# One decoder pair in a single launch: who empties the query blocks, where the decay sums stand, and how wide ff1's moving operand is

## The chip, the cores and the metric

The kernel runs on one core of a Trainium2 chip. The metric is the device time of one execution in microseconds. Three runs of the kernel before took 1574.8, 1575.58 and 1578.62 us; the median is 1575.58 us.

## The reference

The input x is 256 tokens of width 1024 (`SEQ, D = 256, 1024`). It passes a first block of two layers and then a second block of one layer.

A layer of the first block is an RMS norm, a projection, three kinds of mixing (latent attention, selected-key attention, retention), an output projection, and a feed-forward part with `D_FF = 4096`:

```python
hid = square(relu(rms_norm(x) @ w_ff1))     # 256 x 4096
x   = x + hid @ w_ff2
```

The second block projects the normed rows to q, k, v (3 x 768 columns), to the RWKV columns (1824) and to gates (2048). It then computes:

```python
# attention: 3 patterns x 4 heads, scores + bias, softmax, values, w_att_out
w_log = -softplus(-(w0 + tanh(xw) @ w_up)) - 0.5
decay = exp(-exp(w_log)); a = sigmoid(a0 + xa @ a_up); g = sigmoid(xg) @ g_up
# a recurrence over tokens (wkv7_scan): state = state * decay + ... ; out = state @ r
mixed = gates[:D] * y_att + gates[D:] * y_rwkv
x = x + mixed @ w_out
x = x + hierarchical_moe(rms_norm(x))       # 32 experts, top 2 of one group
```

The recurrence is not run token by token. The kernel forms running sums of the log decay within tiles of 128 tokens (the decay sums), takes their exponentials, scales r, k, a, b by them, and turns the recurrence into matmuls and a triangular inverse (the core).

## The kernel before, in words

All five engines run one written-out program each, tied by semaphores. TensorE's results go to eight PSUM banks of 512 words. Every use of a bank is a unit with a name, a bank (or a run of banks) and the engine that empties it, "A" for ScalarE or "V" for VectorE. `layer_plan()` (first block) and `second_plan()` (second block) list the units in TensorE's order. `begin` waits until the bank's previous unit is emptied, `finish` reports it full. So the order is written by hand, and a bank that is emptied late stops TensorE.

Weights come in pieces. SyncE's queue loads a raw piece, ScalarE rounds it to a high part (L1753), GpSimd or VectorE subtracts to get the low part (L878), and TensorE multiplies high x high, high x low and low x high (`product`, L1032 to L1034). A high part may be written only when TensorE has finished the piece 3 places before (first block) or 4 places before (second block).

ff1 works in 8 blocks b of 512 hidden columns for each layer, each block in two units j of 256, each unit in two halves f of 128 columns: for each of 8 k, three matmuls with 128 x 128 weights as the stationary operand and 256 tokens as the moving one. Its units rotate over banks 0 to 3. VectorE empties a unit of 128 x 512 with a maximum against zero (L2365) and squares it (L2367); ScalarE rounds it (L1910), VectorE subtracts (L2373), and ff2 of that block comes one block later. The order on TensorE is ff1(b), ff2(b-1).

The second block starts with `project("rw")`, then the query, key and value columns in five blocks (`QKV_BLOCKS`, four of 512 columns and one of 256, four weight pieces each, two units each: one for each tile of 128 tokens). Units of tile 0 are emptied by VectorE (L2440), units of tile 1 by ScalarE. VectorE first works through the token shift (L2433, L2435, L2437: three operations of 3648 words a partition, which signal `pm_ready`) and only then comes to the first of the query units. The banks are (1, 2, 3, 0), so the fifth unit (block 2) needs the first one emptied.

After the projection the LoRA rows are passed through sigmoid and tanh by ScalarE (L1950, L1951), transposed by TensorE (L1359 to L1361), emptied by ScalarE (L1954, L1955) and multiplied (L1368, L1370, L1371). Then come the gate columns, the transposes of q and k (L1381), and the attention.

The attention has 8 units (two tiles by four heads of three patterns). In round i TensorE makes the scores of i (L1392, L1396), transposes the probabilities of i-1 (L1404), and multiplies the values of i-2 (L1414). VectorE takes the maximum (L2513), ScalarE the exponential (L1976), and it empties the transposed probabilities into one buffer, `att_p`, for which it waits until the values of i-2 are finished.

Behind the attention stand the decay sums: four sums (L1422), eight one-column products in one unit (`sdec`, L1425 and L1426), exponentials on ScalarE (L1992, L1993, L1996), scaling on VectorE (L2529 to L2534, signal `scaled`), 8 units of 4 transposes (L1433), emptied by ScalarE (L2004), the transposed attention (L1440), and its output product `yatt` (L1021). Then the core starts (L1457). GpSimd waits for `scaled`, issues three DMAs of router weights (L2138 to L2140), and forms a product and fills.

The experts (MoE) end the program.

## Time and profile before

| what | value |
|---|---|
| median of three runs | 1575.58 us |
| the profiled execution's own time | 1577.1 us |
| its span | 1575.3 us |
| PE busy | 1489.3 us (95%) |
| DVE busy | 692.7 us (44%) |
| ACT busy | 543.9 us (35%) |
| POOL busy | 443.7 us (28%) |
| mean granted TensorE clock | 0.97 of full speed |

The profile is one execution of the program. PE is TensorE's matmuls, PEld its weight loads, DVE is VectorE, ACT is ScalarE, POOL is GpSimd, SP is SyncE. L12 is line 12 of the kernel. The row of a matmul tells its start and its length, and matmuls overlap: what one costs in a stream is the distance from its start to the next one's. PEclk 1.00 is 2.4 GHz and 0.50 is 1.2 GHz. A bracket at the end of a row is idle time of that engine before it, and who ended it.

### The profile page before, as it was taken

Reading aid. Unit: us, or ns where it says so; the run is one execution under the profiler, and the core shown is the slowest. Engines: PE = TensorE matmul, PEld = TensorE weight load, DVE = VectorE, ACT = ScalarE, POOL = GpSimd, SP = SyncE. Lnnn points to the kernel's source line nnn. Section 1 sums busy time; section 2 is a strip of 40 time slices with the busy share of each in tenths; the row PEclk is TensorE's granted clock in tenths of the full one; section 3 lists DMA queues with packets and bytes.
Section 4 is the critical chain, followed back from the end, with each engine's and each line's share of the span. In section 5 each row is a group of like instructions: output and inputs, shape, how many; then the busy total and the mean of one; then the engine's idle time right before and its main releaser. Section 6 shows DMA issues by size and latency. Waiting matters only on the chain.

```text
span 1575.3 us, 21537 instructions
## 1 busy us (share of the span) xinstructions
PE 1489.3 (95%) x8270; PEld 1087.3 (69%) x8270; DVE 692.7 (44%) x1070; ACT 543.9 (35%) x816; POOL 443.7 (28%) x160
## 2 busy tenths in 40 slices
PE   7989999998989999999979989999899999999997
PEld 6778899987778899987766768974445435444442
DVE  3785465564775475554316625553221111212111
ACT  5546543344646533335434431112111111111111
POOL 3372343434362444437886311100000000000000
PEclk9999999999989999999998979999999999999999
DMA  6442355554332355556763601026599999999995
GB/s 235 141 133 76 108 188 194 180 197 146 121 133 76 134 174 201 180 195 195 235 203 111 227 5 55 1 107 290 215 419 427 429 428 428 425 422 422 428 427 226
DMA packets 44426, 351.91 MB, mean 223 GB/s; under 512 B 5187, under 2 KB 7151, under 8 KB 19759
## 3 DMA queue, kind: packets, MB, share of 16 engines
q1 hardware_dynamic: 43646, 349.37, 58.0%
q8 instruction: 61, 1.00, 0.3%
q10 hardware_dynamic: 576, 1.13, 0.2%
q0 software_dynamic: 112, 0.17, 0.1%
q14 instruction: 31, 0.25, 0.0%
HBM read 347.71 MB, written 1.07 MB: 221 GB/s over the span
## 4 chain that ended last, share of the span: by engine, by line
PE 71%; DVE 8%; DMA 8%; issue 6%; DVEq 2%; ACT 2%; POOL 1%; POOLq 0%; SPq 0%; ACTq 0%
PE psum L1032 13%; PE psum L1033 12%; PE psum L1034 12%; PE psum L1652 12%; DMA ring<-in_w_expert_up 7%; PE psum L1679 5%; PE psum L1021 3%; PE psum L1611 3%; PE psum L1620 1%; PE psum L1100 1%; PE psum L1484 1%; DVE arena L2163 1%; DVE arena L2206 1%; DVE stat L2216 1%; PE psum L1119 1%
## 5 line engine op out<-in xcount | busy, mean ns | idle before, releaser
L878 POOL TENSOR_TENSOR weights_split<-weights_raw,weights_split 128x2048 fp32r<-128x2048 f32 (+4 forms) x108 | 389.6, 3620 | 428.8 <-ACT weights_split L1753 428.7
L1753 ACT ACTIVATE weights_split<-weights_raw 128x2048 fp32r<-128x2048 f32 (+4 forms) x154 | 243.3, 1584 | 283.3 <-PE psum L1034 283.0
L1652 PE MATMUL psum<-ring,arena 128*64 128x512 f32 x976 | 229.2, 604 | 11.2 <-DMA ring<-in_w_expert_up 10.1
L1652 PEld LDWEIGHTS psum<-ring,arena 128*64 128x64 f32 x976 | 74.4, 139 | 148.7 <-issue 148.7
L1032 PE MATMUL psum<-weights_split,h_split 128*128 128x512 f32 (+3 forms) x400 | 154.9, 387 | 15.8 <-DVE arena L2440 6.4
L1033 PE MATMUL psum<-weights_split,h_split 128*128 128x512 f32 (+3 forms) x400 | 153.0, 382 | 0.0
L1034 PE MATMUL psum<-weights_split,h_split 128*128 128x512 f32 (+3 forms) x400 | 152.7, 382 | 0.0
L1032 PE MATMUL psum<-weights_split,hidden_split 128*128 128x512 f32 (+1 forms) x384 | 151.6, 395 | 0.0
L1033 PE MATMUL psum<-weights_split,hidden_split 128*128 128x512 f32 (+1 forms) x384 | 150.1, 391 | 0.0
L1034 PE MATMUL psum<-weights_split,hidden_split 128*128 128x512 f32 (+1 forms) x384 | 149.7, 390 | 0.0
L1032 PE MATMUL psum<-h_split,weights_split 128*128 128x256 f32 x512 | 145.2, 284 | 1.4 <-DVE weights_split L878 1.4
L1034 PE MATMUL psum<-h_split,weights_split 128*128 128x256 f32 x512 | 144.9, 283 | 0.0
L1033 PE MATMUL psum<-h_split,weights_split 128*128 128x256 f32 x512 | 144.9, 283 | 0.0
L878 DVE TENSOR_TENSOR weights_split<-weights_raw,weights_split 128x2048 fp32r<-128x2048 f32 (+2 forms) x46 | 107.1, 2332 | 28.5 <-ACT weights_split L1753 27.8
L1679 PE MATMUL psum<-arena 128*64 128x512 f32 x512 | 113.4, 595 | 0.0
L1032 PEld LDWEIGHTS psum<-weights_split,h_split 128*128 128x128 f32 x400 | 77.4, 194 | 34.2 <-issue 13.2
L1032 PEld LDWEIGHTS psum<-h_split,weights_split 128*128 128x128 f32 x512 | 98.2, 192 | 2.5 <-DVE weights_split L878 1.8
L1033 PEld LDWEIGHTS psum<-h_split,weights_split 128*128 128x128 f32 x512 | 98.2, 192 | 0.5
L1034 PEld LDWEIGHTS psum<-h_split,weights_split 128*128 128x128 f32 x512 | 98.2, 192 | 0.0
L2373 DVE TENSOR_TENSOR hidden_split<-arena,hidden_split 128x512 fp32r<-128x512 f32 x32 | 85.8, 2681 | 15.2 <-ACT hidden_split L1910 15.2
L2794 DVE TENSOR_TENSOR arena<-psum,arena 128x512 f32<-128x512 f32 x16 | 11.1, 692 | 184.0 <-PE psum L1652 184.0
L2804 DVE SCALAR_TENSOR_TENSOR y_parts<-psum,stat,y_parts 128x512 fp32r<-128x512 f32 x32 | 24.0, 751 | 145.8 <-ACT y_parts L2057 145.8
(371 smaller groups left out, 2185.7 us busy)
## 6 DMA issues: line engine op xcount, KB each, us to landing
weights_raw<-in_layer_w SPq DMA_DIRECT2D x94, 1024.0 KB, 4.8
arena<-in_w_expert_down SPq DMA_DIRECT2D x32, 2048.0 KB, 13.3
ring<-in_w_expert_up SPq DMA_DIRECT2D x32, 2048.0 KB, 16.8
ring<-in_w_expert_gate SPq DMA_DIRECT2D x29, 2048.0 KB, 16.1
weights_raw<-in_second_w SPq DMA_DIRECT2D x44, 512.0 KB, 4.2
arena<-in_w_expert_gate SPq DMA_DIRECT2D x3, 2048.0 KB, 9.1
weights_raw<-in_layer_w SPq DMA_DIRECT2D x6, 768.0 KB, 4.1
ring<-in_w_out SPq DMA_DIRECT2D x2, 2048.0 KB, 17.1
```

The source lines that it names most:

```text
L878: eng.tensor_tensor(W.part(j, 1, n), W.raw(j, n), W.part(j, 0, n).bitcast(F32), ALU.subtract).then_inc(W.lo[W.pieces[j][1]], 1)
L1021: ins = pe.matmul(bank[:, 0:n], lhs(i), w[:, i, :], start=(i == 0), stop=(i == k - 1))
L1032: pe.matmul(out, a[0], b[0], start=first, stop=False)
L1033: pe.matmul(out, a[0], b[1], start=False, stop=False)
L1034: return pe.matmul(out, a[1], b[0], start=False, stop=last)
L1100: pe.matmul(bank[:, j * nk:(j + 1) * nk], qT_, kT_, start=True, stop=False)
L1611: ins = pe.matmul(psum[:, 6 + i, kk * P:(kk + 1) * P], xn2[:, t, k * P:(k + 1) * P], take[par][:, t, :, :].rearrange("p j n -> p (j n)"), ...
L1652: ins = pe.matmul(bank[half(j), :], xe[h][:, k, half(j)], w[j][:, k, :], start=(k == 0), stop=(k == KD - 1))
L1679: ins = pe.matmul(bank[half(j), :], hidT[:, f, half(j)], w[j][:, f, c * 512:(c + 1) * 512], start=(f == 0), stop=(f == D_EXP // P - 1))
L1753: act.activation(W.part(j, 0, w), W.raw(j, w), ACT.Copy).then_inc(W.hi, 1)
L2373: dve.tensor_tensor(part[1], hid_sq[i % 4], part[0].bitcast(F32), ALU.subtract).then_inc(hid_ready.sem, 1)
L2804: units.emptied_by(("y", h, c), dve.scalar_tensor_tensor(part[:, 1, :], bank, gate_slot, part[:, 0, :].bitcast(F32), mul, sub))
```

## The change

1. ff1: the three matmuls of one k become two. The high part of the weights multiplies both parts of the tokens in one matmul of 512 columns, into a bank of its own for each f; the low part multiplies the high tokens into the first 256 columns. A unit now has two banks, (0, 1) or (2, 3). VectorE empties it with a sum of two (1024 words in, 512 out), and one operation takes the maximum and squares.
2. Query blocks 0 and 1: both units are emptied by ScalarE.
3. The LoRA rows' sigmoid and tanh stand behind query block 2 on ScalarE, their transposes ahead of the last query block on TensorE.
4. The decay sums and `sdec` stand inside the attention's rounds; `sdec` (the one-column sums) in two halves. The exponential of a sum is written in place in PSUM, and VectorE scales from there. Values of the attention take bank 6 (before 6 and 7). The last attention unit has its own `att_p` and its own banks.
5. The 8 units of transposes are emptied by ScalarE and VectorE in turn; the transposed attention stands behind the sixth; `yatt` takes banks 4, 5, 7, 0 (before 2, 3, 4, 1).
6. The three router DMAs on GpSimd are issued after the second of the core's four starts.

```diff
-        plan += [("ff1", 2 * b + j, (2 * b + j) % 4, "V") for j in range(2)]
+        plan += [("ff1", 2 * b + j, ((0, 1), (2, 3))[j], "V") for j in range(2)]
...
+CUMS = ("cum_excl", "cum_incl") * T
+CUM_AT = {2 * j + 1: j for j in range(len(CUMS))}
...
-    plan += interleave("qkv", PROJ_QKV, (1, 2, 3, 0), "VA")
-    plan += interleave("loraT", T, (4, 5), "A")
+    qkv = [(*unit[:3], "A" if unit[1] < 2 * T else unit[3]) for unit in interleave("qkv", PROJ_QKV, (1, 2, 3, 0), "VA")]
+    plan += qkv[:-T] + interleave("loraT", T, (4, 5), "A") + qkv[-T:]
...
-            plan.append(("PT", i - 1, (4, 5), "A"))
+            plan.append(("PT", i - 1, (4, 5) if i < NA else (0, 1), "A"))
+        if i == 1:
+            plan.append(("sdec", 0, 6, "A"))
         if i >= 2:
-            plan.append(("O", i - 2, (6, 7)[i % 2], "V"))
-    plan += interleave("cum", 2 * T, (0, 1, 2, 3), "AV")
-    plan += interleave("sdec", 1, (4,), "A")
-    plan += interleave("rwT", 8, (5, 6, 7, 0), "A")
-    plan += interleave("attT", 1, (1,), "A")
-    plan += interleave("yatt", 2 * T, (2, 3, 4, 1), "V")
+            plan.append(("O", i - 2, 6 if i <= NA else 4, "V"))
+        if i in CUM_AT:
+            plan.append(("cum", CUM_AT[i], 7, "V"))
+    rwT = interleave("rwT", 8, (2, 3, 5, 7, 0, 1, 6, 2), "AV")
+    plan += rwT[:6] + interleave("attT", 1, (3,), "A") + rwT[6:]
+    plan += interleave("yatt", 2 * T, (4, 5, 7, 0), "V")
...
+        att_p = [area(28736, 768), att_s[0]]
...
-                        ins = product(bank[:, f * SEQ:(f + 1) * SEQ], [part_[:, k, f * P:(f + 1) * P] for part_ in w],
-                                      [hTp[:, which, k, :] for which in range(2)], k == 0, k == KD - 1)
+                        pe.matmul(both.rearrange("p (w s) -> p w s", w=2), w[0][:, k, f * P:(f + 1) * P], hTp[:, :, k, :],
+                                  start=(k == 0), stop=False)
+                        ins = pe.matmul(both[:, 0:SEQ], w[1][:, k, f * P:(f + 1) * P], hTp[:, 0, k, :], start=False, stop=(k == KD - 1))
...
+                if i < 2:
+                    bank = units.begin(("sdec", 0)) if i == 0 else units.bank(("sdec", 0))
+                    for c in range(i * PAIRS // 2, (i + 1) * PAIRS // 2):
+                        pe.matmul(bank[:, c:c + 1], bufR[:, 0, c * P:(c + 1) * P], second("halves")[:, 1:2], start=True, stop=False)
+                        ins = pe.matmul(bank[:, c:c + 1], bufR[:, 1, c * P:(c + 1) * P], second("halves")[:, 0:1], start=False, stop=True)
...
+                if i in CUM_AT:
+                    j = CUM_AT[i]
+                    bank = units.begin(("cum", j))
+                    units.finish(("cum", j), pe.matmul(bank, second(CUMS[j]), bufR[:, j // 2, :], start=True, stop=True))
...
+            act.wait_ge(preproc_done, 1)
             for i in range(NA + 1):
+                if i == 2:
+                    empty(("sdec", 0), sdec, PAIRS, ACT.Exp)
+                if i - 1 in CUM_AT:
+                    j = CUM_AT[i - 1]
+                    bank = units.wait_full(("cum", j))
+                    if CUMS[j] == "cum_incl":
+                        act.activation(bufK[:, j // 2, :], bank, ACT.Exp, scale=-1.0)
+                        act.drain()
+                    act.activation(bank, bank, ACT.Exp).then_inc(cum_exp, 1)
...
-                    if i >= 2:
+                    if 2 <= i < NA:
                         units.wait_full(("O", i - 2))
-                    empty(("PT", i - 1), att_p[:, 0:n], n)
+                    empty(("PT", i - 1), att_p[(i - 1) // (NA - 1)][:, 0:n], n)
...
-                        units.emptied_by(("ff1", i), dve.tensor_scalar(hid_sq[i % 4], bank, 0.0, None, ALU.max), "V")
+                        units.emptied_by(("ff1", i), dve.tensor_reduce(sq.rearrange("p (f s) -> p f s", f=2),
+                                                                       bank.rearrange("p f w s -> p f s w"), AX.X, ALU.add), "V")
                         dve.drain()
-                        dve.tensor_tensor(hid_sq[i % 4], hid_sq[i % 4], hid_sq[i % 4], ALU.mult)
+                        dve.scalar_tensor_tensor(sq, sq, 0.0, sq, ALU.max, ALU.mult)
...
-            for b, (c, w) in enumerate(QKV_BLOCKS):
+            for b, (c, w) in list(enumerate(QKV_BLOCKS))[2:]:
...
+            def scale_rw(j):
+                t = j // 2
+                dve.wait_ge(cum_exp, j + 1)
+                bank = units.bank(("cum", j))
+                if CUMS[j] == "cum_excl":
+                    units.emptied_by(("cum", j), dve.tensor_tensor(bufA[:, t, :], bank, bufA[:, t, :], mul), "V")
+                else:
+                    units.emptied_by(("cum", j), dve.tensor_tensor(bufR[:, t, :], bank, r_[:, t, :], mul), "V")
+                    dve.tensor_tensor(bufB[:, t, :], bufB[:, t, :], bufK[:, t, :], mul)
+                    dve.drain()
+                    dve.tensor_tensor(bufK[:, t, :], bufK[:, t, :], k_[:, t, :], mul)
+                    dve.drain()
+                    dve.sem_inc(scaled, 1)
...
+                if i - 1 in CUM_AT:
+                    scale_rw(CUM_AT[i - 1])
...
+            for j in (1, 3, 5, 7):
+                bank = units.wait_full(("rwT", j)).rearrange("p (c s) -> p c s", c=PAIRS)
+                units.emptied_by(("rwT", j), dve.tensor_copy(rwT[j % 4][:, :, j // 4 * P:(j // 4 + 1) * P], bank), "V")
```

## Rows read from the trace of the kernel before

**Rows 1.** The page's first part: busy time of each engine.

```profile
PE 1489.3 (95%) x8270; PEld 1087.3 (69%) x8270; DVE 692.7 (44%) x1070; ACT 543.9 (35%) x816; POOL 443.7 (28%) x160
```

**Rows 2.** The page's costliest groups: ff1's matmuls (count, busy, mean, idle before).

```profile
L1032 PE MATMUL psum<-h_split,weights_split 128*128 128x256 f32 x512 | 145.2, 284 | 1.4 <-DVE weights_split L878 1.4
```

**Rows 3.** Timeline of TensorE, end of an ff1 block to the next: start, length, operation.

```profile
639.81 0.28 PE L1034 MATMUL psum<-h_split,weights_split 128*128 128x256 f32 x1
...
648.21 0.40 PE L1032 MATMUL psum<-weights_split,hidden_split 128*128 128x512 f32 x1
...
659.12 0.28 PE L1032 MATMUL psum<-h_split,weights_split 128*128 128x256 f32 x1
```

**Rows 4.** Busy time by engine in a stretch of the feed-forward part.

```profile
560.00:640.00 80.00, 80.00 (x503) 72.69 (x502) 45.21 (x27) 31.11 (x22) 33.43 (x8) 1.00 0.57 196
```

**Rows 5.** Timeline of all engines in the feed-forward part.

```profile
603.58 0.69 DVE L2365 TENSOR_SCALAR arena<-psum 128x512 f32<-128x512 f32 x1 [0.92 <-PE psum L1034]
...
605.57 4.62 POOL L878 TENSOR_TENSOR weights_split<-weights_raw,weights_split 128x2048 fp32r<-128x2048 f32 x1 [6.90 <-ACT weights_split L1753]
```

**Rows 6.** Timeline of VectorE: a reduction of 768 words from PSUM.

```profile
900.63 0.96 DVE L2513 TENSOR_REDUCE stat<-psum 128x1 f32<-128x768 f32 x1 [2.94 <-PE psum L1396]
```

**Rows 7.** Timeline of TensorE: it resumes with query block 2.

```profile
792.68 0.77 PE L1032 MATMUL psum<-weights_split,h_split 128*128 128x512 f32 x1 [6.39 <-DVE arena L2440]
```

**Rows 8.** Timeline of GpSimd, the weight pieces of that time.

```profile
781.98 12.10 POOL L878 TENSOR_TENSOR weights_split<-weights_raw,weights_split 128x1024 fp32r<-128x1024 f32 x2
...
794.05 7.09 POOL L878 TENSOR_TENSOR weights_split<-weights_raw,weights_split 128x1024 fp32r<-128x1024 f32 x3
```

**Rows 9.** Timeline of VectorE, the last operation of the token shift.

```profile
785.91 5.96 DVE L2437 TENSOR_TENSOR arena<-arena 128x3648 f32<-128x3648 f32 x1
```

**Rows 10.** Three stretches by engine; the third number from the end is the granted clock.

```profile
794.00:796.00 2.00, 2.00 (x6) 1.52 (x6) 0.00 (x0) 0.00 (x0) 2.00 (x2) 0.50 0.48 172
...
830.00:832.00 2.00, 2.00 (x3) 0.49 (x3) 1.29 (x2) 0.00 (x0) 0.00 (x0) 0.50 0.81 225
...
926.00:928.00 2.00, 2.00 (x3) 0.67 (x2) 0.00 (x0) 0.00 (x0) 0.00 (x0) 0.50 0.00 0
```

**Rows 11.** Timeline of TensorE, the LoRA transposes and products.

```profile
826.19 0.33 PE L1359 MATMUL psum<-shared_c,arena 128*128 128x128 f32 x1 [3.49 <-ACT arena L1951]
...
827.87 2.08 PE L1368 MATMUL psum<-arena 64*128 64x512 f32 x4 [0.81 <-ACT arena L1955]
...
837.76 1.12 PE L1371 MATMUL psum<-arena 32*128 32x512 f32 x2
```

**Rows 12.** Timeline of TensorE from the transposes of q and k to the core.

```profile
883.72 2.78 PE L1381 MATMUL psum<-shared_c,arena 128*128 128x128 f32 x24
...
897.21 1.08 PE L1392 MATMUL psum<-arena,phase_c 128*128 128x512 f32 x2
898.21 1.13 PE L1396 MATMUL psum<-arena 64*128 64x256 f32 x4
...
918.26 0.84 PE L1404 MATMUL psum<-shared_c,arena 128*128 128x128 f32 x6 [1.28 <-ACT arena L1921]
...
922.00 2.82 PE L1414 MATMUL psum<-arena 128*128 128x64 f32 x12 [0.90 <-ACT arena L1921]
924.61 6.20 PE L1422 MATMUL psum<-arena,phase_c 128*128 128x512 f32 x8
930.64 0.28 PE L1425 MATMUL psum<-phase_c,arena 128*128 128x1 f32 x2
...
935.40 5.92 PE L1433 MATMUL psum<-shared_c,arena 128*128 128x128 f32 x32 [2.91 <-DVEq L2535]
...
942.69 7.10 PE L1021 MATMUL psum<-ring,hTs 128*128 128x512 f32 x16 [0.94 <-ACT hTs L1921]
949.73 8.86 PE L1457 MATMUL psum<-arena 64*128 64x128 f32 x80
```

**Rows 13.** Timeline of ScalarE: an exponential of 512 words.

```profile
928.42 0.60 ACT L1992 ACTIVATE arena<-psum 128x512 f32<-128x512 f32 x1 [6.48 <-PE psum L1422]
```

More of the change, by code:

```diff
@@ L1335, in _, with project @@
             _, _, _, part2 = split_products(PW, units, hTp2, second_piece, 0)
-            def project(stage, blocks):
-                for b, (_, w) in enumerate(blocks):
+            def project(stage, blocks, which=slice(None)):
+                for b, (_, w) in list(enumerate(blocks))[which]:
                     for i in range(4):
@@ L1405, in _ @@
                     units.finish(("PT", i - 1), ins)
+                if i < 2:
[3 more added lines that the diff above has]
+                        ins = pe.matmul(bank[:, c:c + 1], bufR[:, 1, c * P:(c + 1) * P], second("halves")[:, 0:1], start=False, stop=True)
+                    if i:
+                        units.finish(("sdec", 0), ins)
                 if i >= 2:
@@ L1441, in _ @@
             units.finish(("attT", 0), ins)
+            turn_rw(range(6, 8))
             w = weights(("att_out", 0))
```

105 lines of the change are left out of this document (41 added, 64 removed).

## The prediction

> **What bounds the kernel now.** I read the page's busy times first: TensorE is busy for 1489.3 us of 1575.3 [rows 1], so a change pays only where it takes work off TensorE or closes one of its gaps. Next came the stretches by engine: in the feed-forward part TensorE is busy for 80.00 of 80 us at clock 1.00, VectorE for 45.21, GpSimd for 33.43 [rows 4]; only TensorE's own work counts there. Then the timeline of TensorE through the second block, where the reader is to look for the brackets: a wait of 6.39 us on VectorE among the query blocks [rows 7], 3.49 and 0.81 us around the LoRA transposes [rows 11], and 1.28, 0.90, 2.91 and 0.94 us between the attention and the core [rows 12]. Last the granted clock: behind each of these gaps it is 0.50, the level of 1.2 GHz [rows 10]. The experts behind this shift as a whole: their loads are released by TensorE's last units of the second block.
>
> **Part 1, ff1.** In a stream a matmul of 256 columns costs (648.21 - 639.81) / 70 = 120.0 ns, one of 512 columns (659.12 - 648.21) / 48 = 227.3 ns [rows 3]. There are 512 groups of three [rows 2]. A group costs 3 x 120.0 = 360 ns before; after, 227.3 + 120.0 = 347.3 ns if the new matmul runs as ff2's do. The saving is 12.7 x 512 = 6.5 us. Bounds: columns alone, at half of 227.3 for the 256 too, give 341 ns, a gain of 9.7 us. The other end: the new moving operand is two runs of 256 words far apart, and so is that of the bias product, which takes 898.21 - 897.21 = 1.00 us for 512 columns where contiguous operands take (949.73 - 942.69) / 8 = 0.88 [rows 12]. At that ratio 227.3 becomes 258, the group 378 ns, and ff1 loses 9.4 us. I take 6.5: ff2 is the neighbour in the same stretch, and the bias product also follows a change from 64 to 128 rows, which can explain its 0.12 us.
>
> The Trainium skill, "TensorE: Matmul & The Clock Gate", section "Back-to-back issue gap", speaks for less: it puts N / 2.4 + 2.5 ns between full-clock matmuls, so that one matmul fewer saves about 2.5 ns; that estimate is 1.3 us for 512 groups. The rows show about 13 ns beyond the columns on each, and the sum goes by them.
>
> VectorE gets more work for each unit: a sum over 1024 words in place of 0.69 us [rows 5]. At the rate of the 768-word reduction (0.96 us [rows 6]) it is about 1.25 us, so +0.6 a unit, +1.1 a block. A block lasts 22.4 us (32 x 0.360 + 48 x 0.2273) and VectorE is busy for 45.21 / 80 = 57% of it, 12.7 us: it becomes 13.8. Even twice the price of the sum is covered. Two pairs of banks in place of four banks: a unit's pair is asked for again two units later, at the earliest 5.5 us after it was full (ff1(0) to ff1(1)), against 1.25 us for the emptying. The weights' chain runs 2% faster: GpSimd's piece starts at 605.57 and takes 4.62 us [rows 5], done at 610.2, and is needed when the two pieces now being multiplied (about 11 us from 603.3) are through, at 614. Cost nothing.
>
> **Part 2, query blocks 0 and 1.** The wait of 6.39 us goes, but another stands behind it. While VectorE does its token shift, GpSimd's low parts take 6.05 us each (two in 12.10) where the next three take 7.09 / 3 = 2.4 [rows 8]. By the count of pieces these two are the first and second of query block 2. So TensorE, which is through with block 1 at 792.68 - 6.39 = 786.3, waits for the first until 788.05, multiplies it (12 matmuls, 2.8 us) until 790.9, and waits for the second until 794.1. From there three pieces at 2.8 us end at 802.5. Before, the block started at 792.68, with ten matmuls at half speed [rows 10], and ended at 805.9: 3.4 us saved if the clock holds. Idle for 5 of 8 us, it hardly will; half speed for one to three pieces' worth costs 1.2 to 3 us. I take 2.0, ends 0.4 and 3.4. The end of the token shift (785.91 + 5.96 = 791.87 [rows 9]) does not move. ScalarE's two more units of 0.7 us fall where it waits for TensorE.
>
> **Part 3, LoRA.** Before, the last query block ends at 822.7 and the gates start at 837.76 + 1.12 = 838.9 [rows 11]: 16.2 us, in which the products run from 827.87 at half speed (11.0 us [rows 10, 11]). After, sigmoid and tanh are done under query block 3, the six transposes cost 6 x 0.116 = 0.7 us at full clock (24 in 2.78 [rows 12]), and their emptying lies under the last query block (5.6 us of matmuls). The products follow without a gap at full clock: six slots of 0.88 us, 5.2 us. Saved 16.2 - 5.2 - 0.7 = 10.3; ends 5 (the clock falls all the same) and 10.8. What moves on ScalarE (2 us with its table load, 1.1 us of copies) stands ahead of weight pieces that TensorE wants 5 us later or more. VectorE's long chain up to the attention, which is done only 1.3 us before the first maximum, hangs on a square root behind gate block 0, so it keeps its place relative to TensorE.
>
> **Parts 4 to 6, attention to core.** In the rounds of the second tile TensorE has no gap, so what moves in costs its own time: four sums at 0.88 and eight one-column products at about 0.2. The first three sums and `sdec` delay the last scores by 2.6 + 1.8 - 0.5 = 3.9 us (0.5 falls into a gap of the first rounds). The fourth sum fills 0.9 of the 1.28 us before the last transposes. Its two exponentials (0.60 each [rows 13]) delay the last probabilities on ScalarE by 1.4 us, but these no longer wait for the values before, so that the 0.90 goes and about 0.1 is left. Then, from the last scores' end at 914.8 + 3.9 = 918.7: values, fourth sum and last transposes by 922.9, values at full clock by 925.5. The first tile's transposes are ready; the second tile's scaling ends at 923.3 + 3 x 0.69 (as [rows 5]) = 925.6. Nine units of transposes at 0.44 take until 929.4, with the attention's emptying under the last two; `yatt` takes 7.0 us [rows 12] to 936.4. The core's first unit now wants the bank of the last `yatt` unit, emptied 0.9 us later: 937.3. Before it started at 949.73 [rows 12]: 12.4 us saved. Of that the sums at half speed [rows 10] and the waits of 2.91 and 0.94 are most. Ends: 8 (low clock through transposes and half of `yatt`) and 13.5.
>
> VectorE's scaling inside a round (0.7 to 2.1 us) stands ahead of emptying the values and of the next maximum. Queued behind it are those two, and TensorE asks for the value bank a round (5.3 us) later; VectorE has 1.8 us of other work a round. The wait for `preproc_done` on ScalarE costs nothing, the first maximum is behind it on VectorE anyway. The router DMAs go into a time when GpSimd waits 39 us for the core's second tile; they are read over 80 us later. In the old place they delayed nothing that TensorE waited for: 0.
>
> **Sum.** 6.5 + 2.0 + 10.3 + 12.4 = 31.2 us. The profiled execution took 1577.1 us, so the same execution becomes 1545.9; it is 1.5 above the median of the runs, which gives 1544.4.
>
> **Rivals.**
> A. The clock stays low from the attention to the core. Here gaps shrink, but the run of transposes grows. Price from rows: 36 transposes at twice 0.11 cost 4 us, and two or three units of `yatt` at half speed 3 to 4: 1551. Against it: of the 32 transposes from 935.40 the last run fast again, the following matmuls at full speed [rows 12], so a stretch of transposes did bring the clock up. The Trainium skill, "TensorE: Matmul & The Clock Gate", section "Part 4: PE-mode transpose", says that transposes don't count as busy for the clock. By that rule this rival would hold; the trace disagrees.
> B. The split operand is no faster than two matmuls of 256 (240 ns) or up to 258: ff1 gains 0 or loses up to 9.4 us: 1551 to 1560. For it only the bias product.
> C. Slower than before: the two-run operand streams at half rate, 455 ns for 512 columns. 512 x (455 + 120 - 360) = 110 us more, less 24.7 from the second block: 1661. It decides from 240 + 24.7 / 0.512 = 288 ns on. Against it: the bias product's operand is of that shape and costs 1.00 us, not 1.76 [rows 12].
> D. The LoRA part does not close (ScalarE comes late with the weights of the gates): 5 us less, 1550. Against it the 5 us of lead above.
>
> **Chances.** Forecast 0.64 (its own range 1540 to 1549), A 0.12, B 0.13, D 0.06, C 0.03, and 0.02 that the second block's gains are eaten by a stall I do not see. About 0.3% (4.7 us) is what a measurement can tell. Faster 0.95, same 0.02, slower 0.03. The range takes A, D and half of B, and downwards 9.7 and 3.4 in place of 6.5 and 2.0: 1538 to 1555.
>
> **What would show it.** ff1: starts of a pair 347 ns apart in sum, TensorE still at 80 of 80 us. Query block 2: two waits on GpSimd (1.8 and 3.1 us) in place of one on VectorE. LoRA: no gap, products in 5.2 us, clock 1.00. From the end of q and k's transposes to the core about 51 us in place of 63.2. The prediction is wrong if the 512-column matmuls stand over 240 ns apart, or if VectorE's row L2373 grows into ff2's start.

## The result, and the profile after

The kernel after the change takes 1560.87 us (median of 4 runs, 1554.68 to 1562.0), the kernel before 1575.86 on the same chip. The ratio is 0.9903, 95% interval 0.988 to 0.9925: faster by 15 us, or 1%. I had forecast 1544.4 with a range of 1538 to 1555. The direction is right, but only half of the 31.2 us came, and the time lies outside the range.

The page's busy times of the kernel after stand against [rows 1]:

```profile
PE 1486.0 (95%) x7758; PEld 1062.8 (68%) x7758; DVE 706.1 (45%) x1072; ACT 545.7 (35%) x812; POOL 444.6 (28%) x160
```

TensorE has 512 matmuls fewer (one for each of ff1's groups), and VectorE has 13 us more. To find where the time went, I set the two timelines side by side and subtract the start of the same operation (us): after each part the lead of the kernel after is known, and its growth is what that part gave.

| milestone | before | after | lead | grown by |
|---|---|---|---|---|
| end of layer 1 | 363.85 | 361.91 | 1.9 | 1.9 |
| last projection unit emptied, at the start of ff1 in layer 2 | 533.76 | 529.72 | 4.0 | 2.1 |
| end of layer 2 | 710.96 | 705.08 | 5.9 | 1.9 |
| last RWKV block emptied | 762.99 | 758.38 | 4.6 | -1.3 |
| end of query block 2 | 805.93 | 799.73 | 6.2 | 1.6 |
| first gate matmul | 838.81 | 823.46 | 15.4 | 9.2 |
| transposes of q and k | 883.72 | 868.53 | 15.2 | -0.2 |
| first matmul of the core | 949.73 | 926.84 | 22.9 | 7.7 |
| second stage of the core | 958.51 | 941.15 | 17.4 | -5.5 |
| last stage of the core | 1036.21 | 1020.19 | 16.0 | -1.4 |
| end | 1575.3 | 1560.2 | 15.1 | -0.9 |

The rows 2.1 and -1.3 belong to code that the change doesn't touch (the mixing of layer 2, the first weights of the second block). Single executions differ there by 1 to 3 us in one place; part of it is that the granted clock is low for a little shorter or longer.

**ff1.** Timeline of TensorE after, the first matmul of ff2, of ff1 and of ff2 again (answers [rows 3]), and the window that answers [rows 4] (its length and the busy time of PE, PEld, DVE, ACT, POOL in us, then granted clock, DMA share, GB/s):

```profile
620.44 0.40 PE L1037 MATMUL psum<-weights_split,hidden_split 128*128 128x512 f32 x1
...
631.38 0.39 PE L1296 MATMUL psum<-h_split,weights_split 128*128 128x512 f32 x1
...
642.67 0.40 PE L1037 MATMUL psum<-weights_split,hidden_split 128*128 128x512 f32 x1
```

```profile
560.00:640.00 80.00, 80.00 (x407) 67.80 (x406) 47.27 (x30) 33.76 (x23) 33.20 (x8) 1.00 0.55 187
```

A block of ff1 takes 642.67 - 631.38 = 11.29 us, a pair 11.29 / 32 = 352.8 ns where 347.3 was forecast; ff2's block takes 10.94 us, a matmul 227.9 ns. TensorE is still busy for 80.00 of 80 us, so it waits for nothing there. VectorE's new sum:

```profile
598.40 1.22 DVE L2386 TENSOR_REDUCE arena<-psum 128x512 f32<-128x1024 f32 x1 [0.54 <-PE psum L1298]
```

It takes 1.22 us (1.25 forecast) and hides behind TensorE's work.

**Query blocks and LoRA.** TensorE's waits in query block 2 (against [rows 7]), and the first LoRA product with the first matmul of the gates (against [rows 11]):

```profile
783.49 0.50 PE L1037 MATMUL psum<-weights_split,h_split 128*128 128x512 f32 x1 [1.82 <-POOL weights_split L883]
...
789.50 0.79 PE L1037 MATMUL psum<-weights_split,h_split 128*128 128x512 f32 x1 [2.96 <-POOL weights_split L883]
```

```profile
817.13 1.13 PE L1378 MATMUL psum<-arena 64*128 64x512 f32 x4
...
823.46 0.51 PE L1037 MATMUL psum<-weights_split,h_split 128*128 128x512 f32 x1
```

The two waits on GpSimd are there, 1.82 and 2.96 us where 1.8 and 3.1 were forecast. The LoRA products follow the last query block without a gap; they take 823.46 - 817.13 = 6.33 us, 1.06 us for each of the six slots. (A row counts two matmuls for each product in f32; the slot of four holds the two products of 64 rows.)

**Attention to core.** Timeline of TensorE from the transposes of q and k to the core (against [rows 12]), and three stretches by engine:

```profile
868.53 2.84 PE L1391 MATMUL psum<-shared_c,arena 128*128 128x128 f32 x24
872.42 0.88 PE L1403 MATMUL psum<-arena,phase_c 128*128 128x384 f32 x2 [1.04 <-ACT arena L1933]
873.23 0.93 PE L1407 MATMUL psum<-arena 64*128 64x128 f32 x6
874.09 0.38 PE L1420 MATMUL psum<-phase_c,arena 128*128 128x1 f32 x2
...
875.21 1.63 PE L1403 MATMUL psum<-arena,phase_c 128*128 128x384 f32 x2
...
913.47 1.55 PE L1432 MATMUL psum<-arena 128*128 128x64 f32 x12 [0.20 <-ACT arena L1933]
...
918.86 7.11 PE L1026 MATMUL psum<-ring,hTs 128*128 128x512 f32 x16
926.84 14.38 PE L1469 MATMUL psum<-arena 64*128 64x128 f32 x80 [0.88 <-DVE arena L2572]
```

```profile
876.00:880.00 4.00, 4.00 (x17) 3.01 (x15) 0.78 (x3) 1.89 (x6) 0.00 (x0) 0.50 1.03 397
...
928.00:932.00 4.00, 4.00 (x27) 4.00 (x26) 2.37 (x4) 0.00 (x0) 2.28 (x2) 0.68 0.96 406
...
936.00:940.00 4.00, 4.00 (x21) 4.00 (x21) 1.83 (x3) 0.00 (x0) 2.90 (x3) 0.50 0.00 0
```

The gaps are as forecast: 0.20 us before the last values, none between the transposes and `yatt`, 0.88 us before the core, where VectorE empties the last unit of `yatt`. The clock is not. It is full through the late part (transposes, `yatt`), where it was low before. But from about 875 to 885 it is 0.50, the level of 1.2 GHz: the score matmuls at 875.21 are rowed at 1.63 us where the same ones are 0.88 at 872.42. And it is 0.50 again from about 929 to 947, so that the core's first stage (the row of 80 matmuls) takes 14.38 us against 8.86 in [rows 12]. The first fall comes 2.4 us behind a gap of 1.04 us, while the first one-column products run; the second comes 2.6 us behind the gap of 0.88 us.

So the theories to test: (G) a gap of about 1 us is what the clock falls behind; (O) the one-column products let it fall; (G2) it takes both together. For ff1's missing 2.8 us: (R) the new operand of two runs costs it, or (S) the alternation of 512 and 256 columns does.

### The profile page after: what moved, and what is told of

It reads as the page before. It is cut to its first block, busy times and chain, and to the rows that moved or that the text cites. A ratio compares the mean times of both kernels' runs of the same rounds, so it can differ in the third digit from the quotient of the medians.

```text
span 1560.2 us, 20516 instructions
## 1 busy us (share of the span) xinstructions
PE 1486.0 (95%) x7758; PEld 1062.8 (68%) x7758; DVE 706.1 (45%) x1072; ACT 545.7 (35%) x812; POOL 444.6 (28%) x160
## 4 chain that ended last, share of the span: by engine, by line
PE 69%; DMA 10%; DVE 7%; issue 6%; DVEq 2%; POOL 2%; ACT 2%; POOLq 0%; SPq 0%; ACTq 0%
PE psum L1664 11%; DMA ring<-in_w_expert_up 10%; PE psum L1037 9%; PE psum L1038 9%; PE psum L1039 9%; PE psum L1296 8%; PE psum L1691 4%; PE psum L1298 4%; PE psum L1026 3%; PE psum L1623 2%; POOL weights_split L883 2%; PE psum L1632 1%; PE psum L1105 1%; PE psum L1496 1%; DVE arena L2184 1%
## 5 line engine op out<-in xcount | busy, mean ns | idle before, releaser
L1664 PE MATMUL psum<-ring,arena 128*64 128x512 f32 x976 | 227.4, 601 | 14.3 <-DMA ring<-in_w_expert_up 13.1
L1296 PE MATMUL psum<-h_split,weights_split 128*128 128x512 f32 x512 | 181.2, 398 | 1.4 <-DVE weights_split L883 1.4
L1298 PE MATMUL psum<-h_split,weights_split 128*128 128x256 f32 x512 | 143.5, 280 | 0.0
L1296 PEld LDWEIGHTS psum<-h_split,weights_split 128*128 128x128 f32 x512 | 96.1, 188 | 25.4 <-DVE weights_split L883 1.9
L1037 PEld LDWEIGHTS psum<-weights_split,h_split 128*128 128x128 f32 x400 | 77.9, 195 | 33.3 <-POOL weights_split L883 11.1
L1298 PEld LDWEIGHTS psum<-h_split,weights_split 128*128 128x128 f32 x512 | 96.6, 189 | 0.5
L1039 PEld LDWEIGHTS psum<-weights_split,h_split 128*128 128x128 f32 x400 | 77.7, 194 | 15.5
L1038 PEld LDWEIGHTS psum<-weights_split,h_split 128*128 128x128 f32 x400 | 77.7, 194 | 14.5
L1039 PEld LDWEIGHTS psum<-weights_split,hidden_split 128*128 128x128 f32 x384 | 73.5, 192 | 13.9
```

The source lines that it names most:

```text
L1037: pe.matmul(out, a[0], b[0], start=first, stop=False)
L1038: pe.matmul(out, a[0], b[1], start=False, stop=False)
L1039: return pe.matmul(out, a[1], b[0], start=False, stop=last)
L1296: pe.matmul(both.rearrange("p (w s) -> p w s", w=2), w[0][:, k, f * P:(f + 1) * P], hTp[:, :, k, :], start=(k == 0), stop=False)
L1298: ins = pe.matmul(both[:, 0:SEQ], w[1][:, k, f * P:(f + 1) * P], hTp[:, 0, k, :], start=False, stop=(k == KD - 1))
L1664: ins = pe.matmul(bank[half(j), :], xe[h][:, k, half(j)], w[j][:, k, :], start=(k == 0), stop=(k == KD - 1))
```

## The experiments

All times are medians, with the 95% interval of the ratio to the kernel before run beside them. "Core at 0.50" means that the core's first stage takes 13 to 15 us in place of 8.8. Experiments 1 to 5, 7 to 9, 14 and 15 edit the kernel after; 6 and 10 to 13 put parts of the change into the kernel before.

**1. The changed kernel once more.**

> The changed kernel once more, for a second profile of it. Facts so far: its first profile is 15.1 us shorter than before's; the core's first 80 products took 14.3 us at clock 0.50 where before took 8.8 us at 1.00, and two rounds of the attention ran at 0.50 too. Theory L (the low clock hangs on the code: gaps and thin matmuls stand at these two places): the same two stretches are at 0.50 again, median 1559 to 1562. Theory P (it is chance how the clock falls, the code only brings it near): at least one of the two stretches differs from the first profile, and the times spread over 4 us or more.

1558.98 us (ratio 0.9873 to 0.9911). The clock is low from about 873 to 883 and from 927 to 945. Both falls come again in this kernel.

**2. `yatt`'s banks.**

```diff
-    plan += interleave("yatt", 2 * T, (4, 5, 7, 0), "V")
+    plan += interleave("yatt", 2 * T, (4, 5, 0, 7), "V")
```

> The changed kernel with banks 4, 5, 0, 7 for yatt in place of 4, 5, 7, 0, so that the core's first unit no longer waits for the last yatt unit. Theory G (the gap of 0.88 us ahead of the core makes the clock fall there): gap gone, the first 80 products at 1.00 in 8.8 us, median 6 to 8 us less than the changed kernel's (1553 to 1555). Rival (the products over 64 rows alone let it fall): gap gone, products still at 0.50, gain 1 us or less.

1551.97 us (0.9832 to 0.9869). The core's first products in its trace, and a stretch of them:

```profile
922.42 7.85 PE L1469 MATMUL psum<-arena 64*128 64x128 f32 x71
```

```profile
926.00:930.00 4.00, 4.00 (x42) 4.00 (x40) 3.24 (x6) 0.00 (x0) 3.46 (x4) 1.00 0.77 330
```

There is no bracket, and the clock is 1.00. One swapped bank is worth 7 us against experiment 1, of which the gap itself is 0.9. The fall in the attention stays (about 871 to 881).

**3. The one-column products two rounds later.**

```diff
-                if i < 2:
+                if i in (2, 3):
```

(with bank 5 for them and bank 4 for the first tile's transposed probabilities)

> The changed kernel with the two halves of the one-column products in rounds 2 and 3 of the attention in place of 0 and 1 (own bank 5, probabilities of the first tile in bank 4). Theory G2 (the gap of 1.04 us before the attention and the one-column products right behind it together let the clock fall): clock 1.00 through the attention, about 4.5 us less up to the end of the attention. Rival O (one-column products count as next to nothing wherever they stand): 0.50 for some 8 us again, only later. What the core does is left open by both.

1556.61 us (0.9863 to 0.99), but its five times are 1549.22 and then 1555.69 to 1557.52. The first one's profile has the core's first stage at full clock. But the clock fell in the attention, for 7 us behind a gap of 1.18 us, before any of the one-column products, which start at 880.19 here:

```profile
872.00:876.00 4.00, 3.70 (x12) 2.53 (x13) 1.45 (x5) 2.66 (x6) 0.00 (x0) 0.54 1.02 414
876.00:880.00 4.00, 4.00 (x12) 1.79 (x11) 0.10 (x1) 1.34 (x5) 0.00 (x0) 0.60 1.04 386
```

That is not what G2 said (1.00 through the attention), nor what O said (a fall later, with the products). A second profile of the same program:

> The kernel with the one-column products in rounds 2 and 3 once more, one look. Its first profile (1549.2 us) shows the core's first stage at clock 1.00, while four of its five timed runs took 1555.7 to 1557.5. Theory: it stands on the edge, and in those runs the clock falls behind the gap before the core, which costs 5.5 to 7 us; a profile of a run near 1556 then shows that stretch at 0.50. If a profile near 1556 shows the core at 1.00, the difference lies elsewhere. If the run is again near 1549, nothing is told.

1558.69 us, with the attention at 1.00 this time. One stretch of the core in the first profile (1549.22), and then in the second:

```profile
924.00:928.00 4.00, 4.00 (x41) 4.00 (x40) 2.87 (x5) 0.00 (x0) 1.97 (x2) 1.00 0.91 381
```

```profile
924.00:928.00 4.00, 4.00 (x25) 4.00 (x24) 1.68 (x3) 0.00 (x0) 3.43 (x3) 0.50 0.80 342
```

The same program, the same gap of 0.87 or 0.88 us, once without the fall and once with it, and 9 us between the two times. Moving the thin products out of the first rounds settles neither place.

**4. The one-column products widened to 128 columns** (the extra columns hold sums that nobody reads).

```diff
-  pe.matmul(bank[:, c:c + 1], bufR[:, 0, c * P:(c + 1) * P], second("halves")[:, 1:2], start=True, stop=False)
+  pe.matmul(bank[:, c * P:(c + 1) * P], bufR[:, 0, c * P:(c + 1) * P], phase_c[:, o + 1:o + 1 + P], start=True, stop=False)
```

(and the second of each pair in the same way; ScalarE reads column 0 of each 128)

> The changed kernel with 128 columns in each of the eight one-column products (127 of them unused). Their distance is 0.22 us at full clock for one column, and the weight load should still set it, so they take the same time. Theory O (thin matmuls don't keep the clock up): with 128 columns the attention stays at 1.00 and ends about 4.5 us earlier. Rival G2 (the gap before, not the width): still 0.50 from about 875 to 885 us.

1546.61 us (0.98 to 0.9834), the five runs within 3.7 us. Timeline of TensorE, and a stretch in the attention and in the core:

```profile
868.61 0.88 PE L1403 MATMUL psum<-arena,phase_c 128*128 128x384 f32 x2 [1.14 <-ACT arena L1934]
869.42 0.93 PE L1407 MATMUL psum<-arena 64*128 64x128 f32 x6
870.29 0.49 PE L1421 MATMUL psum<-phase_c,arena 128*128 128x128 f32 x2
...
871.28 0.81 PE L1403 MATMUL psum<-arena,phase_c 128*128 128x384 f32 x2
...
918.67 8.83 PE L1470 MATMUL psum<-arena 64*128 64x128 f32 x80 [0.88 <-DVE arena L2574]
```

```profile
876.00:880.00 4.00, 4.00 (x26) 2.97 (x26) 1.79 (x6) 1.56 (x5) 0.00 (x0) 1.00 1.04 387
...
922.00:926.00 4.00, 4.00 (x42) 4.00 (x41) 3.24 (x6) 0.00 (x0) 3.46 (x4) 1.00 0.59 252
```

The two halves (four products each) take 871.28 - 870.29 = 0.99 us and 0.90 us at 128 columns. At one column and full clock a half takes 0.81, as the first profile of experiment 3 shows:

```profile
880.19 0.28 PE L1420 MATMUL psum<-phase_c,arena 128*128 128x1 f32 x2
...
881.00 0.86 PE L1432 MATMUL psum<-arena 128*128 128x64 f32 x6
```

So the widening costs 0.1 to 0.2 us a half. The clock stays at 1.00 behind both gaps. From the transposes of q and k (864.65) to the core it is 54.0 us, against 66.0 before. Against the profile of experiment 1, 4.4 us of the gain lie between the attention's first scores and the core, and 6.9 in the core up to its gap of 0.78 us (956.67), where the code is the same; why the clock holds there too, the edit doesn't tell.

**5. Both.**

> The changed kernel with both edits: yatt's banks (4, 5, 0, 7), so that the gap of 0.88 us before the core goes, and the eight one-column products widened to 128 columns. Theory O (the thin products let the clock fall, and the gap before the core only finds a clock that is already near falling): the clock is at 1.00 in both places already with the wide products alone (1546.6 us), so the bank order adds only its own gap, 0.9 us: 1545.7. Theory G (each gap has its own price and they add): 1559 - 7 (bank order alone) - 12.4 (wide alone) = 1540. A third way: the core's own chain of triangular inverses on GpSimd is what ends last once the clock is up (a wait of 0.9 us on GpSimd at L1487 stands in the trace of the bank order alone), so the 0.9 us goes into that wait and the time is 1546.6 as before.

1547.46 us (0.9809 to 0.985), no different from the wide products alone. G's sum of 1540 falls: where the clock holds, the bank order is worth less than a run's noise. A wait of 0.86 or 0.88 us on GpSimd follows in the core's second stage in both traces, so it does not take up the gap's 0.9 us, and the third way isn't shown either.

**6. ff1 alone**, on the kernel before.

> The kernel before with the ff1 edit alone. If its gain is 512 x (360 - 352.8) ns = 3.7 us, as the milestones of the two traces say, the median is 3.7 us below the kernel before (ratio 0.9976, about 1571.5). If ff1 saved the 6.5 us forecast and another edit took 2.8 us of it back in the same stretch, it is 1568.7 (0.9959). If the second block's changes are worth more or less with ff1 unchanged (the two interact through the weights' chain), the difference of 15 us is not the sum of 3.7 and the rest, and this run shows it with the later runs of the other parts alone.

1569.96 us (0.9947 to 0.9976), 4 to 8 us less than before: the interval doesn't separate 3.7 from 6.5. Its trace does: ff1's block takes 11.29 us and ff2's 10.94 in it. A block of ff1 is 0.23 us shorter than before (11.52), 3.7 us in all 16, and one of ff2 is 0.03 longer (10.91 before), which takes 0.5 back. What the total shows beyond that isn't traced to a place.

**7. ff1 with a contiguous operand.**

```diff
-  pe.matmul(both.rearrange("p (w s) -> p w s", w=2), w[0][:, k, f * P:(f + 1) * P], hTp[:, :, k, :],
+  pe.matmul(both.rearrange("p (w s) -> p w s", w=2), w[0][:, k, f * P:(f + 1) * P], hTp[:, 0, k // 2 * 2:k // 2 * 2 + 2, :],
```

> The changed kernel with ff1's 512-column moving operand taken from two neighbouring high parts, which are one run of 512 words, in place of the high and the low part of one k, which are two runs of 256 words; the product of high weights and low tokens is so left out. Theory R (two runs cost what the new matmul takes over ff2's: 0.236 against 0.227 us): the pair falls from 353 to about 345 ns and the kernel gains 512 x 8.5 ns = 4.3 us against the changed kernel, 1555. Theory S (the price is that of alternating 512 and 256 columns, or of this stationary operand; the runs cost nothing): the pair stays at 353 ns, 1559.

```profile
620.28 0.40 PE L1037 MATMUL psum<-weights_split,hidden_split 128*128 128x512 f32 x1
...
631.23 0.39 PE L1296 MATMUL psum<-h_split,weights_split 128*128 128x512 f32 x1
```

The block ends 11.29 us later (642.52), as in the changed kernel: R falls, two runs cost nothing. The whole takes 2030.11 us, which says nothing of ff1: the kernel leaves out the product of high weights and low tokens, other activations reach the router, and the experts' first product runs 2000 matmuls in place of 976.

**8. ff1 grouped by width.**

```diff
                     for k in ks:
                         pe.matmul(both.rearrange("p (w s) -> p w s", w=2), w[0][:, k, f * P:(f + 1) * P], hTp[:, :, k, :],
                                   start=(k == 0), stop=False)
+                    for k in ks:
                         ins = pe.matmul(both[:, 0:SEQ], w[1][:, k, f * P:(f + 1) * P], hTp[:, 0, k, :], start=False, stop=(k == KD - 1))
```

> The changed kernel with ff1's matmuls of one half f in another order: first the eight of 512 columns, then the eight of 256. Theory S (alternating the two widths costs): the eight of 512 columns stand 227 ns apart and the eight of 256 columns 117 to 120, a pair costs 345 ns, 4 us less than the changed kernel: 1555. Theory R (the two runs cost it, wherever the matmul stands): 236 and 120 ns, a pair 353 to 356 ns, the same or up to 1.5 us more: 1559 to 1561. With either theory the order could also cost: each group of three products is now eight matmuls apart in the bank, which takes nothing from TensorE.

```profile
610.62 1.98 PE L1296 MATMUL psum<-h_split,weights_split 128*128 128x512 f32 x8
612.43 1.11 PE L1299 MATMUL psum<-h_split,weights_split 128*128 128x256 f32 x8
...
621.76 0.40 PE L1037 MATMUL psum<-weights_split,hidden_split 128*128 128x512 f32 x1
...
632.67 0.62 PE L1296 MATMUL psum<-h_split,weights_split 128*128 128x512 f32 x2
```

1556.23 us (0.9863 to 0.99). A block takes 621.76 - 610.62 = 11.14 us, a pair 348.1 ns, and eight matmuls of 512 columns take 612.43 - 610.62 = 1.81 us, 226 ns each; ff2's block is 10.91 again, as in the kernel before. Alternating the two widths costs 4.7 ns a pair, most of the 5.5 over the forecast, so S holds; its 345 ns are not reached. 16 blocks x (0.15 + 0.03) = 2.9 us.

**9. Wide products and grouped order.**

> The changed kernel with the two edits that helped: the one-column products widened to 128 columns, and ff1's matmuls grouped by width (eight of 512, then eight of 256). If the two act in different places and add: 1546.6 (wide alone) less 16 blocks x 0.19 us = 3.0: 1543.6, and the core's first stage at clock 1.00. If the grouped order's gain was luck of the clock and not the 0.15 us of ff1 and 0.03 us of ff2 that its trace shows for each block: 1546.6.

1545.65 us (0.9792 to 0.9833), the core at 1.00 in the profile. It beats both kernels, but isn't told apart from the wide products alone; 3 us less, as expected, is not shown.

**10. Parts 2 and 3 alone**, on the kernel before.

> The kernel before with the edits of the query blocks and the LoRA rows alone (parts 2 and 3). By the milestones of the two traces these gave 1.6 and 9.2 us, so 10.8 us off the kernel before: about 1564.8, and the attention starts 10.8 us earlier with nothing changed behind it. If they owe part of that to ff1's or the attention's edits: less. The forecast had 12.3 for the two.

1567.88 us (0.993 to 0.9973): 7.2 less than before, where 10.8 was expected. The ten times stand in two groups, and the profile was of the lower one (1558.49). Hence:

> The kernel with the edits of the query blocks and the LoRA rows alone once more, one look. Its timed runs stand in two groups, 1557.6 to 1558.5 (two of ten) and 1566.5 to 1571.5 (eight); the profile in hand is of the fast group and shows only 8 us of lower clock (0.77 and 0.80) between the attention and the core. Theory: in the slow group the clock is 0.50 there, as in the kernel before, through sums, transposes and half of yatt, and the time is near 1568. If a profile near 1568 shows that stretch at 1.00, the cost lies elsewhere.

1567.01 us. The same stretch in the lower group, and then in this one:

```profile
912.00:916.00 4.00, 2.67 (x19) 2.11 (x17) 1.25 (x2) 1.67 (x5) 0.00 (x0) 1.00 0.00 0
```

```profile
912.00:916.00 4.00, 3.10 (x15) 2.91 (x15) 0.28 (x1) 0.81 (x1) 0.00 (x0) 0.50 0.00 0
```

The clock makes part of the difference between the two groups: from the last values to the transposes of the scaled rows it is 926.14 - 913.19 = 13.0 us in the slower one and 917.59 - 907.95 = 9.6 in the other. The transposes of q and k also start 4.1 us later there (874.54 against 870.46), in code ahead of it.

**11. Parts 4 to 6 alone.**

> The kernel before with the edits of attention to core alone (parts 4 to 6). Theory: the one-column products let the clock fall inside the first rounds (4.7 us), and the gap before the core finds it low again (5.5 us), so that of 12.4 us forecast about 2 are left at the core's end, less what the experts lose (0.6): 1573 to 1575, no measurable change. Rival: the clock falls in the changed kernel because of what the other edits do to the load ahead of the attention (LoRA products and gates without a gap); then it holds here, and the kernel gains 10 to 12 us: 1564.

1574.94 us (0.9972 to 1.0018): no change in the median (one of the twelve runs took 1558.85, at a mean granted clock of 0.981 where the others have 0.967 to 0.971), though the stretch from the transposes of q and k to the core is 9 us shorter than before (885.54 to 942.73). A stretch in the attention and one in the core:

```profile
896.00:900.00 4.00, 4.00 (x9) 1.89 (x9) 0.00 (x0) 0.79 (x3) 0.00 (x0) 0.50 1.04 387
...
948.00:952.00 4.00, 4.00 (x24) 4.00 (x23) 1.69 (x3) 0.00 (x0) 1.26 (x1) 0.50 0.12 49
```

**12. Parts 4 to 6 with wide products.**

> The kernel before with the edits of attention to core alone, and the eight one-column products widened to 128 columns. Theory O (the thin products are what let the clock fall, and the rest of the forecast for parts 4 to 6 was right): from the transposes of q and k to the core 54.0 us as with the wide products in the changed kernel (66.0 before), the core's first stage at 1.00: 12 us off the kernel before, 1563. Rival: with LoRA's gaps and low clock still ahead of the attention the widening helps less; if the clock falls as in the run of parts 4 to 6 alone, no change against before, 1575.

1571.11 us (0.9954 to 0.9996), between the 1563 of theory O and the 1575 of its rival. The rows show why:

```profile
892.00:896.00 4.00, 3.58 (x22) 2.56 (x21) 0.78 (x3) 3.07 (x9) 0.00 (x0) 1.00 1.02 401
...
944.00:948.00 4.00, 4.00 (x24) 4.00 (x24) 2.08 (x3) 0.00 (x0) 1.46 (x2) 0.50 0.18 78
```

The attention is at 1.00, and the stretch takes 54.0 us as in experiment 4 (884.98 to 939.00). But the core is at 0.50 behind its gap. Theory O's second half (the gap alone does nothing) is wrong.

**13. The same without the gap.**

> The kernel before with the edits of attention to core, the wide products, and yatt's banks (4, 5, 0, 7), so that TensorE has no gap ahead of the core. With the wide products alone the attention came out as forecast (54.0 us from the transposes of q and k to the core, 66.0 before), but the core's first stage still ran at 0.50, so that 1571.1 were left of 1563. Theory G2 (the gap of 0.88 us before the core is the trigger of the core's fall, whatever stands in the attention): the core's first stage is at 1.00 in nearly all runs, and the time is 1571.1 - 7 - 0.9 = 1563. Rival (the fall there belongs to the place in the program or to the work after the gap): no change, 1570.

```profile
937.03 8.19 PE L1465 MATMUL psum<-arena 64*128 64x128 f32 x74
...
975.04 2.00 PE L1514 MATMUL psum<-arena 128*128 128x64 f32 x16 [0.78 <-DVE arena L2624]
```

```profile
940.00:944.00 4.00, 4.00 (x41) 4.00 (x41) 3.37 (x5) 0.00 (x0) 3.53 (x3) 1.00 0.93 397
...
988.00:992.00 4.00, 4.00 (x19) 3.77 (x19) 1.27 (x3) 0.00 (x0) 0.00 (x0) 0.50 0.00 0
```

1576.29 us (0.9935 to 0.9997; five of the twelve runs took 1559.1 to 1569.1, the other seven 1575.9 to 1580.4). The core's first stage is at 1.00, as G2 says. But the clock now falls from about 978 to 1012, 34 us, behind a later gap of the core (0.78 us, which is in every kernel here); behind the gap of 0.87 us on GpSimd that comes before it, at 947.84, it held. Both forecasts of the time were wrong. In the profile the edit has moved the fall; the slower runs have a mean granted clock of 0.967 to 0.969, the five faster ones 0.972 to 0.979.

**14. Wide products, ff1 as before.**

> The changed kernel with the wide products and with ff1 as before. In the changed kernel with the wide products the core ran at 1.00 behind the same gap of 0.88 us; without the edits of ff1, query blocks and LoRA it ran at 0.50. If what tells them apart is the shape of the work ahead of the attention (LoRA's gaps), the core is at 1.00 here too, and the time is 1546.6 + 3.7 = 1550.3. If it is a matter of when the gap comes, so that a shift of 3.7 us by ff1 changes it, the core can be at 0.50 in some or all runs, and the time is 1555 to 1557.

1554.97 us (0.9844 to 0.9884), and the time would suit a fall in the core. The trace says otherwise: attention and core are at 1.00. The 4.7 us over 1550.3 come earlier: the ff1 of layer 2 starts at 533.93 against 528.84 with the wide products alone, of which ff1 in layer 1 explains 1.9. The other 3.2 arise in the mixing of both layers, and 2.5 more arise in the first query blocks, from the token shift (774.41 against 767.02) to the emptying of block 2 (804.51 against 794.67); neither edit touches that code.

**15. All three edits.**

> The changed kernel with all three: wide products, yatt's banks (4, 5, 0, 7), grouped order in ff1. The candidate for the best version: no gap before the core, so that its clock hangs on nothing. If the three add: 1546.6 - 3.0 - 0.9 = 1542.7; if the bank order is worth nothing where the clock holds anyway (its own run with the wide products took 1547.5): 1544 to 1546.

1546.01 us (0.9789 to 0.9823), five runs at 1545.0 to 1546.9 and one at 1553.14. The profile is of that one. It shows a fall of 3 us in the attention and one of 13 us in the core, behind the gap of 0.78 us; so removing the gap before the core does not make the clock safe:

```profile
872.00:876.00 4.00, 4.00 (x17) 2.92 (x16) 0.71 (x2) 2.16 (x4) 0.00 (x0) 0.57 1.02 414
...
964.00:968.00 4.00, 4.00 (x21) 4.00 (x20) 0.42 (x1) 0.00 (x0) 0.00 (x0) 0.50 0.00 0
```

## Why the prediction was wrong

**The step that failed** is "Parts 4 to 6": 12.4 us forecast, about 1 left (7.7 at the core's start, then -5.5 and -1.4). Its sum of work was right to 0.4 us. With the clock held, the stretch takes 54.0 us (experiments 4 and 12; 53.0 in 5, where the gap before the core is gone), a gain of 12.0. What failed was the assumption that the clock holds, in two places:

- The new one-column products in the first rounds. I priced them as work (1.8 us, about right) and kept the rounds at full clock. In the six profiles with one-column products in rounds 0 and 1 the clock fell there every time, for 7 to 17 us; with 128 columns it fell in one of seven, for 3 us, and with the products in later rounds in one of two, for 7 us. A gap of 1.04 to 1.18 us stands ahead in all fifteen. In the four profiles that have the rounds as before (kernel before, experiments 6 and 10) it is 0.95 to 1.08 us, and the clock holds in the first rounds. So thin work behind the gap makes the fall far more likely and longer, but it takes no thin work: two of the thirteen profiles without it fell too.
- The gap of 0.88 us before the core. I forecast it, and priced it at its own length. In eleven profiles with this gap the clock fell in the core's first stage in six; in the four without it, in none, though in two of these it fell behind the later gap of 0.78 us instead. The price of a fall there is 5.5 us in the first stage and 1.4 behind it, 7 us for 0.88. Experiment 1 against 2 shows the same 7 us in the medians.

Rival A (clock low from attention to core, 1551) names the right mechanism in the wrong place: it feared the transposes. They run at full clock here. That its 1551 is nearer to the measured time than my forecast is luck. The Trainium skill, "TensorE: Matmul & The Clock Gate", section "Part 4: PE-mode transpose", says that transposes don't count as busy; the 36 transposes behind the attention run at 1.00 into `yatt` in the kernel after and in experiment 4, so the trace again disagrees. The Trainium skill says on the same page, section "A second HAM failure mode: psum-queue depth-cycling", that small and frequent idle times between groups of matmuls can make the clock swing between its levels. The falls here, behind single gaps of 0.78 to 1.18 us, go the same way, and I should have weighed it for the new gap.

**ff1** was mis-sized: 3.7 us in place of 6.5. The pair costs 352.8 ns, not 347.3. ff2's price holds for a 512-column matmul among its like (226 ns in experiment 8), and alternating with 256 columns adds 5 ns a pair. ff2's block is 0.03 us longer beside it, 0.5 us in all, which is not in the 3.7. The operand of two runs, the whole reason for my lower bound and rival B, costs nothing (experiment 7). VectorE's work and the banks hid as said. From the Trainium skill, "TensorE: Matmul & The Clock Gate", section "Back-to-back issue gap", I had the estimate of 1.3 us. The rows show 7.2 ns saved for each group and 11.9 in the grouped order, so neither the 2.5 ns of that section nor my 12.7.

**Query blocks**: 1.6 us measured, 2.0 forecast, both waits as worked out. **LoRA**: 9.2 measured, 10.3 forecast. The gap closed and the clock held; a slot costs 1.06 us, where I had taken 0.88 from `yatt`. The bias product in my own rows (1.00 us for 512 columns) was nearer. Alone, these two parts gave 7.2 us by the medians and not 10.8. In the profile of experiment 10's slower group the transposes of q and k start 9.2 us earlier than before (874.54 against 883.72); part of the difference is clock in places that vary from run to run, the rest isn't traced.

**The rest**: the experts' stretch is 0.9 us longer, with 13.1 us of waits for weights where 10.1 were before. I had priced that at nothing. No run here tells whether the router's three DMAs have to do with it; it was not tried. In sum, of 31.2 forecast: 2.8 less in ff1, 0.4 and 1.1 less in parts 2 and 3, 11.6 less in parts 4 to 6, 0.9 in the experts, which leaves 14.4; with 0.6 from unchanged code it is 15.0, and the measured lead is 15.1. (The 0.6 are 2.1 - 1.3 - 0.2 of the table.)

What stays open: why the same gap brings the clock down in one execution and not in the next, and in one program in most runs and in another in none seen. The experiments show that it depends on more than the gap and the work right behind it. Experiments 4 and 12 have the same code from the attention on and differ in it. Nor does a fall in the attention decide the core's: in experiment 7 and the first profile of experiment 3 the clock fell in the attention and held in the core's first stage, in the second profile and in experiment 12 it was the other way round. No experiment sets the time at which a gap comes by itself.

## What to carry to other kernels

Price a gap of TensorE of about 1 us not at its length but at what stands behind it: 1 us of waiting cost up to 7 here, and removing it can move the fall to a later gap, so judge by many runs and by the granted clock in the stretch, never by one total. Do not place very thin matmuls behind a gap, where wide ones cost nearly the same: here 128 columns took 0.1 to 0.2 us more than one for four products, and gave 12 us in the changed kernel (4 where parts 4 to 6 stood alone, experiments 11 and 12). In a stream that is bound by TensorE, group matmuls of one width.

## What the runs showed of the hardware that I had not expected

- The clock falls in stretches in which TensorE is busy throughout: 4.00 of 4 us at 0.50 behind the 0.88 us gap, for 17 us in the kernel after. Behind the gap of 0.78 us in experiment 13 it stays down for 34 us.
- Two executions of one program can differ by 9 us (experiment 3, two profiles) or 18 us and more (experiment 13, 1559 to 1577). In experiment 13 the mean granted clock of these runs is 0.979 and 0.967.
- Within a half, products of one column and of 128 columns stand equally far apart at full clock, 0.22 to 0.23 us (two matmuls each).
- Alternating 512 and 256 columns costs 352.8 ns a pair, grouped by eight 348.1. Whether the 512 words of the moving operand are one run or two changes nothing (11.29 us a block both ways).
- A slot of 512 columns in f32 costs 1.06 us in LoRA's stream (817.13 to 823.46), whether it holds one product of 32 or 128 rows or two of 64, and 0.88 in `yatt`'s.
